# A seventh paired pair of up features in each FFN layer, with its turned rows prepared four features earlier

## What is computed

```python
def conv_ffn(h, w_up, conv_w, conv_b, w_down):     # D_FF = 2816
    u = h @ w_up                                   # 1024 -> 2 * 2816
    up = jnp.pad(u, ((0, 0), (CONV_W - 1, 0), (0, 0)))
    u = sum(up[:, j:j + seq] * conv_w[j] for j in range(CONV_W)) + conv_b
    a, b = u[..., :D_FF], u[..., D_FF:]
    return (jax.nn.silu(a) * b) @ w_down
```

## Time and profile before

| | |
|---|---|
| median of 3 runs | 2112.48 us (2112.15 to 2113.44) |
| span of the profiled execution | 2111.6 us |
| PE busy | 2094.3 us, 99% |
| DVE, ACT, POOL busy | 1358.7, 1088.4 and 1115.7 us |
| mean granted TensorE clock | 0.999 |
| chain that ended last | PE 91%, DVE 6%, issue 2%, ACT 2% |

### The profile page before, as it was taken

The page is one execution under the profiler, slowest core; times in us unless marked ns, Lnnn a source line. Parts: engine busy times, 40 slices in busy tenths (PEclk is TensorE's granted clock), DMA queues, the critical chain, the costliest instruction groups (busy, mean ns, idle before and its releaser), DMA issues.

```text
span 2111.6 us, 29835 instructions
## 1 busy us (share of the span) xinstructions
PE 2094.3 (99%) x11235; PEld 1801.2 (85%) x11235; DVE 1358.7 (64%) x2284; ACT 1088.4 (52%) x1750; POOL 1115.7 (53%) x662
## 2 busy tenths in 40 slices
PE   9999999999999999999999999999999999999999
PEld 7867889889888888888899898888888888899998
DVE  7973786767634445467776684897567325785773
ACT  6564654654433424346546545445877535645642
POOL 3514666874534343435758834655433554838843
PEclk9999999999999999999999999999999999999999
DMA  4203223333322222222232324322212342333232
GB/s 167 70 11 93 97 92 100 101 101 106 119 85 90 85 91 84 92 80 89 92 101 93 117 85 174 110 80 72 78 61 71 91 140 90 100 100 101 90 108 93
DMA packets 57677, 200.69 MB, mean 95 GB/s; under 512 B 6400, under 2 KB 7168, under 8 KB 57280
## 3 DMA queue, kind: packets, MB, share of 16 engines
q1 hardware_dynamic: 56816, 197.46, 29.1%
q10 hardware_dynamic: 720, 1.34, 0.2%
HBM read 194.32 MB, written 4.19 MB: 94 GB/s over the span
## 4 chain that ended last, share of the span: by engine, by line
PE 91%; DVE 6%; issue 2%; ACT 2%; DMA 0%; SPq 0%; DVEq 0%; POOL 0%; ACTq 0%
PE ps L404 21%; PE ps L406 21%; PE ps L405 21%; PE ps L707 6%; PE ps L709 6%; PE ps L708 6%; PE ps L434 2%; PE ps L433 2%; PE ps L432 2%; PE ps L2444 1%; PE ps L1837 1%; DVE SC L1051 1%; DVE X L1024 0%; PE ps L2429 0%; PE ps L2456 0%
## 5 line engine op out<-in xcount | busy, mean ns | idle before, releaser
L382 POOL TENSOR_TENSOR WL<-WS,WH 128x1024 fp32r<-128x1024 f32 (+1 forms) x276 | 652.2, 2365 | 710.4 <-ACT WH L372 709.8
L404 PE MATMUL ps<-H,WH 128*128 128x512 f32 (+2 forms) x1488 | 580.8, 390 | 1.7 <-DVE H L612 1.1
L405 PE MATMUL ps<-H,WH 128*128 128x512 f32 (+2 forms) x1488 | 578.0, 388 | 0.0
L406 PE MATMUL ps<-H,WL 128*128 128x512 f32 (+2 forms) x1488 | 577.9, 388 | 0.0
L372 ACT ACTIVATE WH<-WS 128x1024 fp32r<-128x1024 f32 (+2 forms) x278 | 286.6, 1033 | 296.7 <-PE ps L406 167.1
L404 PEld LDWEIGHTS ps<-H,WH 128*128 128x128 f32 (+1 forms) x1488 | 279.1, 188 | 60.4 <-DVE H L612 2.7
L406 PEld LDWEIGHTS ps<-H,WL 128*128 128x128 f32 (+1 forms) x1488 | 279.0, 187 | 58.2
L405 PEld LDWEIGHTS ps<-H,WH 128*128 128x128 f32 (+1 forms) x1488 | 279.2, 188 | 54.5
L1213 POOL TENSOR_TENSOR WL<-WS,WH 128x512 fp32r<-128x512 f32 x162 | 214.2, 1333 | 197.1 <-ACT WH L830 195.3
L404 PE MATMUL ps<-G,WH 128*128 128x512 f32 x496 | 193.6, 390 | 2.0 <-DVE G L2163 1.4
L707 PE MATMUL ps<-G_long,WH 128*128 128x256 f32 x672 | 191.4, 285 | 2.6 <-DVE X L1024 2.1
(11 more groups left out here) (328 smaller groups left out, 4060.2 us busy)
## 6 DMA issues: line engine op xcount, KB each, us to landing
WS<-in_w SPq DMA_DIRECT2D x337, 512.0 KB, 3.5
WS<-in_w SPq DMA_DIRECT2D x24, 384.0 KB, 3.1
xs<-X SPq DMA_DIRECT2D x1, 2048.0 KB, 6.7
X<-xs SPq DMA_DIRECT2D x8, 256.0 KB, 3.7
out<-X SPq DMA_DIRECT2D x8, 256.0 KB, 2.0
X<-in_sg SPq DMA_DIRECT2D x1, 1344.0 KB, 6.0
X<-in_x ACTq DMA_DIRECT2D x4, 256.0 KB, 6.0
X<-in_x SPq DMA_DIRECT2D x4, 256.0 KB, 5.8
```

The lines of the kernel that those rows point to most:

```text
L382: e.tensor_tensor(lo, raw, hi.bitcast(F), ALU.subtract).then_inc(*P.sig("w_lo", i))
L404: e.matmul(out, lh, rh, start=start, stop=False)
L405: e.matmul(out, lh, rl, start=False, stop=False)
L406: return e.matmul(out, ll, rh, start=False, stop=stop)
```

## The change

Pair 5 joins `UP_PAIRED`, in all three layers. The quarters of turned rows, which were begun by ACT in iterations 1 to 4 and finished by DVE in iterations 2 to 5, for pair 7, are now begun in iterations 0 to 3 and finished in iterations 1 to 4. On POOL quarter q moves from iteration q+3 to iteration q+1. On ACT the high part moves ahead of `tap2` of the partner feature, and `scaled(q)` from the end of iteration q+1 to the end of iteration q. On DVE `turned_lo(q)` moves from iteration q+2 to q+1.

```diff
--- before.py
+++ after.py
@@ -652,7 +652,7 @@
     return P.G(7168 + lo * 3072 + (p - 16) * T)
 
 
-UP_PAIRED = (7, 11, 13, 15, 17, 19)
+UP_PAIRED = (5, 7, 11, 13, 15, 17, 19)
 
 
 def f_tap(P, z):
@@ -946,6 +946,8 @@
             if p == z - 1:
                 forms_2(p - 1)
                 break
+            if 1 <= p < 5:
+                turned_hi(p - 1)
             if ahead:
                 act_form(P, e, pair, "s3", P.raw(pair, "a21"))
                 part(pair, "p1", f_part(P)[:, 0:256], P.ps(("up", L, FT + p + 1))[:, 0:256], "a11")
@@ -960,11 +962,9 @@
                 P.hi_n = P.index.get(("ups", L, p + 1, 1), 0) + 1
             elif not paired:
                 hi_to(P, e, P.ahead(("up", L, FT + p), True))
+            if p < 4:
+                scaled(p)
             first_forms(p + 2)
-            if 2 <= p < 6:
-                turned_hi(p - 2)
-            if 1 <= p < 5:
-                scaled(p - 1)
         for name in ("s4", "a22"):
             act_form(P, e, (L, g, 0), name)
         for mp in range(1, 4):
@@ -1156,9 +1156,9 @@
             forms_2(p - 1)
             tap1(FT + p)
             tap0(FT + p)
+            if 1 <= p < 5:
+                turned_lo(p - 1)
             forms_3(p - 1)
-            if 2 <= p < 6:
-                turned_lo(p - 2)
         last = z - 1
         for mp in range(4):
             pair, more = (L, g, mp), (L, g, mp + 1)
@@ -1253,8 +1253,8 @@
                 pool_up_pair(P, e, L, p)
                 continue
             lo_to(P, e, P.ahead(("up", L, p)) - LEAD)
-            if 3 <= p < 7:
-                pool_turned(P, e, L, p - 3)
+            if 1 <= p < 5:
+                pool_turned(P, e, L, p - 1)
             lo_to(P, e, P.ahead(("up", L, FT + p)) - LEAD)
         for mp in range(4):
             pair = (L, g, mp)
```

## The result

The changed kernel takes 2226.27 us (median of four runs, 2225.25 to 2229.04); the kernel before, run beside it on the same chip, 2112.32 us (four runs, 2112.15 to 2113.44). The ratio is 1.0542, with a 95% interval from 1.0527 to 1.0557: 114 us slower. Predicted were 2227 us, from 2199 to 2240. The size came out, but two terms behind it were wrong and nearly cancelled: the waits are 10.5 us shorter than forecast, the clock costs 9.4 us more. The rows show where.

What follows compares the result with a forecast made beforehand. PE, at work 99% of the span, was taken as the bound. To 2111.6 us the prediction added 95.4 of waits less the saved product and 19.6 of slow clock, 2226.6, and with 0.9 to the median said 2227, range 2199 to 2240.

Steps and rivals of the forecast that it cites:

- the saved product: Pairing pair 5 takes 10.07 us of PE instead of 10.88, gaining 0.81 us a layer if nothing waits.
- the pair's added work: The seventh pair's extra work on ACT, DVE and POOL lies beside PE and was costed at nothing.
- Wait 1: PE ahead of feature 23 waits for its weights' low part, behind POOL's quarter 0: 11.6 us a layer.
- Waits 2 to 4: PE ahead of features 24, 25 and 26 waits for weights' low parts behind POOL's quarters 1 to 3: 5.0, 5.6, 3.7 us.
- the contention: POOL's sums slowed beside DVE's L1118, adding 1.0, 0.4 and 0.7 us to the waits of features 24, 25 and 26.
- Wait 5: Product s1 of pair 5 waits for quarter 3's `t_lo`: 6.7 us a layer; E is when feature 26 finishes.
- The clock: PE's clock halves after four of the five waits a layer, 1.6 us each: 6.5 us a layer, 19.6 in all.
- Rival 3: Clock falls after all five waits and sums contend at their most: 2236 us or more; chance 0.12.
- rival 2: Waits as forecast, but the clock stays up except perhaps after the long first one: 2201 to 2216 us; chance 0.27.
- Rival 4: Only the fifth wait is there, because POOL's lead covers its quarters: 2130 us; chance 0.06.
- rival 5: No wait appears and the change does what its arithmetic says: 2110 us; chance 0.03.

Runs made afterwards that it cites:

- e5_both_moves: Changed kernel with POOL's quarters one to two low parts later and the last quarter's high and low part ahead of feature 26's steps: 2133.21 us.
- e8_weights_first: Changed kernel with the whole turned-row chain earlier and, in ACT's iterations 1 to 3, the next weights' high part first: 2118.34 us.
- e6_first_scaling_early: Changed kernel with only quarter 0's scaling moved on ACT, from behind the second tap to directly behind the row of norms: 2202.08 us.
- e4_busy_waits: Changed kernel with matmuls whose result is overwritten filling PE's five waits a layer, nothing else changed: 2202.37 us.
- e10_quarters_2_3_early: e8_weights_first with quarters 2 and 3 earlier on POOL and their scalings one iteration earlier on ACT: 2118.21 us.
- e9_early_chain_six_pairs: e8_weights_first with pair 5 formed as an ordinary pair, leaving only the earlier chain of turned rows: 2112.37 us, ratio 1.0001 to the kernel before.

## Why the prediction was right, and where it was not

**What bounds the kernel, what is gained.** Right: PE without waits, so only waits count. The 0.8 us a layer of the saved product are in the account, and they never showed in a time: no order tried with seven pairs came below the kernel before. That the pair's added work costs nothing held in the changed kernel, where the long waits cover it; where they are gone it costs more than the pair saves, 15.2 us of PE's waits in e5_both_moves and 5.5 in e8_weights_first.

**Wait 1** was forecast at 11.6 us and is 11.6, step by step: the first sum was to start at 222.5 and starts at 220.91, with the 1.56 us by which this run is early 222.47. e6_first_scaling_early shows its cause.

**Waits 2 to 4** were forecast at 5.0, 5.6 and 3.7 and are 4.3, 5.2 and 4.0. The chain was right, and what was mis-sized is the contention, forecast at 1.0, 0.4 and 0.7 and measured at 0.3, nothing and 1.0: with these the prediction's own 4.0, 5.2 and 3.0 give 4.3, 5.2 and 4.0. In wait 2 L1241 took 1.05 us at 237.58 beside L1118 (236.81). In waits 3 and 4 of layer 0:

```profile
255.65 0.73 POOL L1241 TENSOR_TENSOR turned_whole<-GF 128x256 f32<-128x256 f32 x1 [10.18 <-ACT GF L896]
...
271.25 1.65 DVE L1118 TENSOR_TENSOR turned_cut<-turned_whole,turned_cut 128x1024 fp32r<-128x1024 f32 x1
...
271.76 1.73 POOL L1242 TENSOR_TENSOR turned_whole<-GF 128x256 f32<-128x256 f32 x1
```

At 255.65 L1118 is over (254.12 to 255.34), and the sum takes its 0.73. In the other rows the two take turns: the later of the two ends about its own time, less some 0.1 us, after the earlier has ended. L1118 ends at 238.03 and the sum at 238.63, 0.60 later; at 271.76 L1118 ends at 272.90 and the sum at 273.49, 0.59 later; at 240.62 L1118 ends at 241.75 and the sum at 242.35, again 0.60. So the price is what the other engine's instruction still has to run, and the 1.0 that the prediction read at 240.62 was that of a L1118 which had itself been held up, to 2.59 us, by POOL's L382 ahead of it. The GPSIMD Engine Reference of the Trainium skill, Key points, says that GpSimd contends for its SBUF interfaces with VectorE instructions that have two inputs in SBUF. This case's runs agree, at a price between 0.3 and 1.1 us for a POOL instruction.

**Wait 5** is the term that was furthest off: "POOL begins the pair's sums ... 5.5 us before E; s2 is summed ... E + 0.8", with `tap2` at E + 3.4 and L1118 at 1.93 to 2.59. Measured, with E = 284.54: POOL's sum ended near 283.5 and ACT rounded it at 283.53, E - 1.0, since feature 26 ran on a slow clock and gave the chain 1.7 us; `tap2` started at 286.45, E + 1.9; and L1118 at 288.70 took 1.22 us. The durations of before, 1.93 to 2.59, were already stretched by POOL: the shortest of the twelve L1118 of before took 1.93, and 1.22 is what it takes with POOL idle. 1.5 us from the place of `tap2` and 0.7 to 1.4 from L1118: 4.0 in place of 6.7. So waits and clock, the two terms that the prediction added, were coupled: the slow clock ahead of pair 5 hides part of pair 5's wait, and e4_busy_waits gives it back (5.3 us at full clock).

**The clock** was forecast at four of five drops of 1.6 us. It fell after all five, at 1.5 to 2.6 us each, 29 us and not 19.6, and e4_busy_waits shows that it is the waits that do it. In layers 1 and 2 it stayed down for longer behind the first wait (0.50 over the 5.26 us from 1013.17). The Trainium skill's page TensorE: Matmul & The Clock Gate (HAM oscillation) says, of a kernel whose bursts are shorter than the waits between them, that the clock drops each time; here PE works for 8.5 us and more between two waits, and it drops each time too, with five windows of five between 0.50 and 0.78. The one row from which the prediction took its price is no firm ground: the same wait left the clock at 1.00 in the changed kernel's profile. Rival 3 had this part right, and missed upward in the waits; rival 2, the clock that stays up, would have given 2201 to 2216 and is excluded by the windows.

**The rivals.** Rival 4 (only the fifth wait) and rival 5 (none) needed quarter 0's scalings before 210.9; they stand at 219.52.

**The sum.** 97.8 us of waits forecast and 87.3 measured, 19.6 us of clock forecast and 29.0 measured: 117.4 against 116.3, less 2.4 both times. The mechanism and the places of the waits were right; that the time lies within 1 us is luck, since the two errors have opposite signs.

**What stays open** is whether any order feeds s2 of pair 5 in time. POOL has eleven operations of some 1.25 us for a pair, 13.8 us in all, while PE needs 10.07 us; before, POOL led by 8.5 us at pair 7 (267.58 to 276.05). e10_quarters_2_3_early has 7.5 us and loses 3.5 of it to ACT and DVE; an order that gives pair 5 the lead of pair 7 without those two was not found, and the best of the seven-pair kernels, 2118.2, stays 6 us above before. With no wait at pair 5 it would gain 2.4 us, 0.11%, hardly more than the half width of the narrowest interval here (0.09%, e9_early_chain_six_pairs).

## What to carry to other kernels

Before moving work to another place of an in-order queue, write down for each moved instruction what it waits for and who is queued behind it: here four short sums ahead of a weight's low part, four times a layer, cost 98 us, though POOL was idle half the time. A wait of TensorE costs its length and then the slow clock behind it, and the two don't simply add when the next wait hides the slow stretch. A duration read beside another engine is an upper bound, so look for the same instruction alone before it goes into a sum.

## What the runs showed of the hardware that was not expected

- In the changed kernel the clock fell after each of the fifteen waits of 3.8 us and more, though PE had worked without a gap for 8.5 us and more before them.
- After a short wait it fell in some places and not in others. Behind the wait of 1.43 us in the attention it reads 0.52 in the profile of before and 1.00 in that of the change. Behind the waits of 1.8 us in e8_weights_first it reads 0.81 in layer 0, where pair 5 took 13.65 us (253.03 to 266.68), 10.07 + 1.85 and 1.7 more, and 1.00 in layer 1, where it took 12.26 (1006.28 to 1018.54), 0.3 more. What decides between the two is open.
- After the fifth wait, in layer 0, it fell only when PE had been back for 1.4 us.
- Overwritten matmuls in the waits took all of it away (clock 1.000) and were worth 24 us in e4_busy_waits.
- DVE's 128x1024 operation with two SBUF inputs takes 1.22 us alone and up to 2.6 beside POOL; POOL's of 0.73, 1.29 and 1.28 us take 1.73, 2.28 and 2.38 beside it. They take turns: the one that starts later ends some 0.6 us (POOL's of 0.73) or 1.1 us (DVE's of 1.22, POOL's of 1.29) after the other.
